# A ring of fifteen weight slots instead of fourteen, with the shared expert's units loaded and used in the first three expert groups

## The reference

```python
scores = sigmoid(h @ w_router)
_, top_e = lax.top_k(scores + b_router, TOP_K)              # 8 of 64 experts
...
return (silu(xb @ w_eg[e]) * (xb @ w_eu[e])) @ w_ed[e]      # each routed expert
...
shared = (jax.nn.silu(h @ w_sg) * (h @ w_su)) @ w_sd        # the shared expert, all tokens
return (routed + shared).reshape(B, S, D)
```

## Time and profile before

| what | value |
|---|---|
| median of 3 runs | 1431.17 us (1430.2 to 1432.47) |
| span of the profiled execution | 1432.0 us |
| mean granted TensorE clock in it | 0.990 of full speed |
| PE busy, share of the span | 1383.3 us, 97% |
| read from HBM | 509.89 MB, 357 GB/s over the span |
| expert stage of layer 0 on PE | about 252 to 731 us |
| expert stage of layer 1 on PE | about 948 to 1429 us |

### The profile page before, as it was taken

One profiled execution on the slowest core, in us unless ns is written; L12 is line 12 of the kernel. 1 busy time (PEld: TensorE's weight loads), 2 busy tenths in 40 slices (PEclk: granted clock), 3 DMA queues, 4 the chain that ended last, 5 costly groups with the idle time before them and its releaser, 6 DMA issues.

```text
span 1432.0 us, 20559 instructions
## 1 busy us (share of the span) xinstructions
PE 1383.3 (97%) x8361; PEld 792.2 (55%) x8361; DVE 321.0 (22%) x776; ACT 267.2 (19%) x531; POOL 31.5 (2%) x79
## 2 busy tenths in 40 slices
PE   5999999999999999999989989999999999999997
PEld 2777866455544444444458868854554444444442
DVE  1330523111011111111133477241010111111111
ACT  2211513111011111111033365231101111111100
POOL 5000000000100000000000000000010000000000
PEclk9999999999999999999999989999999999999999
DMA  9999299899999999999998500149999999999996
GB/s 375 414 420 421 122 371 400 351 393 421 364 420 421 421 421 420 421 422 420 421 417 321 232 30 2 66 181 381 420 370 408 420 421 422 420 421 421 421 420 278
DMA packets 71599, 512.30 MB, mean 358 GB/s; under 512 B 8240, under 2 KB 8432, under 8 KB 9552
## 3 DMA queue, kind: packets, MB, share of 16 engines
q1 hardware_dynamic: 70560, 509.64, 86.6%
q0 software_dynamic: 800, 1.25, 0.3%
q10 hardware_dynamic: 144, 0.08, 0.0%
HBM read 509.89 MB, written 1.05 MB: 357 GB/s over the span
## 4 chain that ended last, share of the span: by engine, by line
PE 90%; DMA 5%; DVE 3%; ACT 1%; issue 1%; SPq 0%; DVEq 0%; ACTq 0%
PE PS L932 23%; PE PS L922 13%; PE PS L940 12%; PE PS L536 12%; PE PS L956 11%; DMA ring<-in_w_exp 4%; PE PS L563 3%; PE PS L691 2%; PE PS L968 2%; PE PS L1804 1%; DMA ring<-in_w_ada_units 1%; PE PS L515 1%; PE PS L547 1%; PE PS L977 1%; PE PS L648 1%; PE PS L672 1%
## 5 line engine op out<-in xcount | busy, mean ns | idle before, releaser
L932 PE MATMUL PS<-ring,scratch 128*32 128x512 f32 (+2 forms) x2176 | 355.6, 597 | 7.3 <-DMA ring<-in_w_exp 5.8
L932 PEld LDWEIGHTS PS<-ring,scratch 128*32 128x32 f32 (+2 forms) x2176 | 111.6, 123 | 244.0 <-issue 242.2
L922 PEld LDWEIGHTS PS<-scratch,u 128*128 128x128 f32 x1600 | 183.0, 192 | 38.7 <-issue 36.8
L922 PE MATMUL PS<-scratch,u 128*128 128x128 f32 x1600 | 192.5, 278 | 1.4 <-ACT scratch L1156 1.4
L940 PE MATMUL PS<-ring,scratch 128*32 128x512 f32 (+2 forms) x1088 | 182.2, 596 | 2.6 <-DMA ring<-in_w_exp 1.4
L956 PE MATMUL PS<-scratch 128*128 128x512 f32 x384 | 172.7, 592 | 0.0
L1292 DVE TENSOR_TENSOR scratch<-PS,gate_row 128x512 f32<-128x512 f32 x100 | 69.2, 692 | 461.8 <-PE PS L940 461.8
L536 PE MATMUL PS<-ring,uT 128*128 128x256 f32 x672 | 150.4, 383 | 0.0
L1164 ACT ACTIVATE scratch<-PS 128x256 f32<-128x256 f32 x50 | 19.2, 384 | 675.4 <-PE PS L932 675.4
L536 PEld LDWEIGHTS PS<-ring,uT 128*128 128x128 f32 x672 | 127.1, 191 | 22.6 <-issue 5.0
L940 PEld LDWEIGHTS PS<-ring,scratch 128*32 128x32 f32 (+2 forms) x1088 | 52.6, 122 | 122.6 <-issue 120.9
(11 more groups left out here) (332 smaller groups left out, 854.4 us busy)
## 6 DMA issues: line engine op xcount, KB each, us to landing
ring<-in_w_exp SPq DMA_DIRECT2D x384, 1024.0 KB, 16.7
ring<-in_w_ada_units SPq DMA_DIRECT2D x56, 1024.0 KB, 17.8
ring<-in_w_in_a_units SPq DMA_DIRECT2D x12, 1024.0 KB, 26.8
ring<-in_w_cmp_units SPq DMA_DIRECT2D x8, 1024.0 KB, 27.0
ring<-in_w_sh_units SPq DMA_DIRECT2D x6, 1024.0 KB, 13.5
ring<-in_w_kv_b_units SPq DMA_DIRECT2D x6, 1024.0 KB, 22.6
ring<-in_w_o_a_units SPq DMA_DIRECT2D x4, 1024.0 KB, 12.4
ring<-in_w_in_b_units SPq DMA_DIRECT2D x4, 1024.0 KB, 10.8
```

Of the source, the lines that this page charges most:

```text
L922: mm = pe_.matmul(PS[:, bank, i * w:(i + 1) * w], u[:, t, k * P:(k + 1) * P], hot[:, t, :], start=(t == 0), stop=(t == NT - 1))
L932: mm = pe_.matmul(PS[places, GU, :], x[:, kk, places], gate_and_up, start=(kk == 0), stop=(kk == KC - 1))
```

## The change

SLOTS goes from 14 to 15. SHARED_AT goes from groups 4, 5, 6 to groups 0, 1, 2. In the list, and in SP's code that follows it, a shared unit now stands at the head of its group, ahead of the gate-and-up units (and ahead of the wait for `order_ready` in group 2). Where PE uses the shared unit within its group is not changed.

```diff
-SLOTS = 14
+SLOTS = 15
...
-SHARED_AT = [4, 5, 6]
+SHARED_AT = [0, 1, 2]
...
     for g, group in enumerate(GROUPS):
+        out += [(f"shared{layer}", j) for j in range(3) if SHARED_AT[j] == g]
         out += [("gate_up", layer, g, half, i) for half in range(2) for i in range(len(group))]
-        out += [(f"shared{layer}", j) for j in range(3) if SHARED_AT[j] == g]
         out += [("down", layer, g, i) for i in range(len(group))]
...
                 for g, group in enumerate(GROUPS):
+                    for j in range(3):
+                        if SHARED_AT[j] == g:
+                            load(f"shared{layer}", j)
                     if group[0] < STATIC:
                         which = [slice(r, r + 1) for r in group]
...
                             unit(gate_up_unit(layer, g, i, half), w[:, half:half + 1, :])
-                    for j in range(3):
-                        if SHARED_AT[j] == g:
-                            load(f"shared{layer}", j)
                     for i, w in enumerate(weights):
                         unit(down_unit(layer, g, i), w[:, 2:3, :])
...
-            first = [AT["gate_up", layer, 0, 0, 0] for layer in range(2)]
+            first = [AT[f"shared{layer}", 0] for layer in range(2)]
```

## The result

The changed kernel takes **1483.86 us** by median (1477.52 to 1489.63, 4 runs) against 1431.82 us for the kernel before (1430.2 to 1439.09): a ratio of 1.0355, 95% interval 1.033 to 1.038. The prediction had the direction and most of the mechanism, but 1465 us, with a range that ended at 1474. The loss is 52 us and not 34.

The account below looks back on a forecast made before the run. The weights' DMA queue at about 421 GB/s was taken to end both expert stages. Median 1431.2 plus 34 us of queue delay (between 29.6 and 35.9), small parts 0, gave 1465 us; range 1455 to 1474.

Parts of the forecast that it names:

- places 15, 22 and 29: Units of an expert stage's load list, counted from 0, that take the slots of the three shared units.
- the three pauses and their times: Layer 0's queue idles from 257 to 272 us, then some 5 us up to 297 and up to 322.6.
- the balance of bytes: Expert stages: units landed at the third release and units still to move give 18.6 and 17.3 us late, together 35.9.
- The 34: Total delay of both expert stages taken for the forecast, in us, between the ends 29.6 and 35.9.
- the plain row of units: Expert stages as unbroken units from the issue of place 29 plus landing: 15.2 and 14.4 us late, together 29.6.
- The stated range of 1458 to 1471: Main case, chance 0.85: spanned by its two ends and the 2.5 us of the start.
- POOL's multiplication takes 4.78 us ... so it ends near 262 ... nothing: Shared down unit: it lands by 257, POOL ends near 262, PE wants it at 315.7; cost 0.
- In layer 1 ... three more fit in as well. Both cost nothing: Before the stages: three shared units load ahead of the order in both layers, at no cost.
- the delay is passed on as it is: After layer 0's expert stage: later units follow the last down in time, so its delay neither grows nor shrinks.
- The rival "Larger": Expert stages: PE's waits before groups bring half clock, four long ones a layer adding 14 us: 1479; chance 0.04.

Follow-up runs that it names:

- the repeat: The changed kernel timed again with no edit, against the kernel before: 1483.70 us, ratio 1.0353.
- the two kernels with POOL held back: Changed kernel with POOL's shared multiplication waiting for the item tables: 1472.14 us; the same plus seven useless matmuls in the attention's wait: 1471.49 us.
- The changed kernel with the fill: Changed kernel with POOL's multiplication held back and seven useless matmuls in the second attention's wait: 1471.49 us, 1.0278 against the kernel before.

## Why the prediction was wrong

*Right.* That the weights' queue ends both stages; that SP stands still at places 15, 22 and 29 until a shared unit has been used; the three pauses and their times; that no pause comes back after the third. Taking the place in the list away, or releasing the slots sooner, brings 27 to 40 us back; moving the list alone, with the old groups, costs 34. PE's waits for experts' weights were to rise to some 40 us and are 35.1; the last downs of layer 0 were to begin near 741 and begin at 744.98, 1.9 us of which stem from before the stage.

*Mis-sized: the queue's share.* By the balance of bytes the last downs of layer 0 were to come 18.6 us late and the second half of layer 1 17.3; the stages grew by 19.8 and 18.5. The balance was 2.4 us low in all. The 34 was lower still because it leaned towards the plain row of units (29.6), which I had myself found to land too low in the old stages. That term, 34, measured 38.3 in the first profile (37.4 to 39.1 in the repeat and the two kernels with POOL held back). The stated range of 1458 to 1471 has a slip too: its upper end by the terms named is 1431.2 + 35.9 + 2.5 = 1469.6.

*Failed: "POOL's multiplication takes 4.78 us ... so it ends near 262 ... nothing".* For layer 0 it holds that PE waits for nothing (POOL ends at 263.87). For layer 1 the step was not worked out: the unit lands about 10 us before the gate row is ready, so POOL's start is set by the gate row, and that falls beside DVE's routing chain, on which PE waits. This cost 5.5 us, and holding POOL back took them away.

*Failed: "In layer 1 ... three more fit in as well. Both cost nothing".* The fifteenth unit takes the slot of the last unit before the stage, and so meets the router's weights. This cost 1.3 us in the profile. PE's wait for the router's weights is 1.7 to 1.8 us in every profile in which all three shared units are listed ahead of the order, and 0.3 to 0.4 in all the others. No run was made to price it by itself.

*Failed: "the delay is passed on as it is".* The stretch from the key/value stream to layer 1's router grew by 8.4 us in the first profile, through the clock, and by 2.5 us in the repeat; with POOL held back it was 2.5 us shorter than before. So this loss belongs to the execution and comes and goes. Fifteen slots alone meet it too. How much of it the change causes stays open. The rival "Larger" looked for the half clock in the expert stages, where it does occur (0.79 in 422 to 438 us, behind a wait of 6.21 us) while the queue, which sets the end, runs on at 420 GB/s. In the attention nothing hides it. That this rival's 1479 us lies near the lower heap is luck: its 14 us were to come from waits that cost next to nothing.

Together 38.3 + 5.5 + 1.3 make 45, or 1477 us, at the lower edge of the lower heap (1477.5 to 1480.6, mean 1478.5). The other 7 us of the median go with a lower granted clock (0.973 to 0.978 in the upper heap against 0.982 to 0.987), but which spells make them is shown for one profile only.

## What to carry to other kernels

When a ring's loads are issued in order, what counts is not how early a unit is loaded but how long its slot is held, since every later load queues behind that release: list a unit next to its use, or use it as soon as it is listed. When work moves earlier on one engine, look at what it will then run beside in every layer, not only in the first. And where times fall into two heaps, read the granted clock of each before a median is compared: the one slot more was worth nothing by median, and 4.4 us beside the kernel before with the same fill (1426.78 against 1431.13) once a 2 us wait was filled; both together gave 0.4 to 0.7%.

## What the runs showed of the hardware

TensorE stayed at half clock for about 34 us while it was busy nearly throughout (31.9 of 32 us at a mean granted clock of 0.51 with fifteen slots alone); work alone did not bring it back at once. The spell began behind a wait of only 2.16 us, in a stretch where PE had already been idle in part (busy 15.9 of the 20 us from 848 to 868 in the changed kernel, at a clock of 1.00). Behind the same wait in the kernel before the spell lasted about 7 us, so the wait does not set its length. Filling that single wait kept the clock at 1.00 from 849 to 881 us in the profile of the fifteen-slot kernel, and no run of its upper heap (1433 us and more) was seen again in 18; a spell ahead of the filled wait remained. The changed kernel with the fill still had two of six runs above the rest. What decides whether and for how long a run meets the spell, and where the remaining slow runs lose their time, stays open.

A DVE instruction with SBUF operands alone was held up to the end of a POOL instruction of 2.38 us that ran beside it (0.42 us became 2.30), while one that reads PSUM and one SBUF tile was not (0.29 us).
